# The half swap of a rotary embedding: one transfer set on ScalarE's queue in place of a product on TensorE

## The reference

```python
h = _layernorm(x) * (1.0 + scale) + shift            # scale, shift, gate = silu(c) @ w_ada + b_ada
p = h @ w_in[l]
u_f, z_f, cq, ckv, k_r, z_a = split(p)               # 1024, 1024, 512, 256, 64, 1024 columns
y_f = _fourier_mix(u_f, w_fmix[l]) * silu(z_f)
q = _rmsnorm(cq) @ w_q_b[l]                          # 8 heads of 128 + 64
kv = _rmsnorm(ckv) @ w_kv_b[l]                       # 8 heads of 128 + 128
q_rope = _apply_rope(q[..., 128:], cos, sin)         # 8 heads, 64 each
k_rope = _apply_rope(k_r, cos, sin)                  # one, shared by the heads
y_a = softmax((q_nope k_nope + q_rope k_rope) / sqrt(192)) v * silu(z_a)
x = _layernorm(ALPHA * x + gate * (concat(y_f, y_a) @ w_out[l]), g, b)

def _apply_rope(x, cos, sin):
    x1, x2 = split(x, 2, axis=-1)                    # halves of 32
    return concatenate([x1 * cos - x2 * sin, x2 * cos + x1 * sin])
```

## Time and profile before

| what | value |
|---|---|
| median of three runs | 1576.99 us (1576.58 to 1578.29) |
| span of the profiled execution | 1576.4 us |
| TensorE busy | 1505.3 us, 95% of the span |
| VectorE busy | 1064.3 us, 68% |
| ScalarE busy | 708.5 us, 45% |
| mean granted TensorE clock | 0.988 |
| moved by DMA | 345 MB, 219 GB/s over the span |
| the ten rotations' products on TensorE | 20 records (two each), 379 ns the median one |

### The profile page before, as it was taken

One profiled execution on the slowest core, in us unless ns is written; L12 is line 12 of the kernel. 1 busy time (PEld: TensorE's weight loads), 2 busy tenths in 40 slices (PEclk: granted clock), 3 DMA queues, 4 the chain that ended last, 5 costly groups with the idle time before them and its releaser, 6 DMA issues.

```text
span 1576.4 us, 25483 instructions
## 1 busy us (share of the span) xinstructions
PE 1505.3 (95%) x10143; PEld 1332.0 (84%) x10143; DVE 1064.3 (68%) x1729; ACT 708.5 (45%) x1216; POOL 40.7 (3%) x58
## 2 busy tenths in 40 slices
PE   5999999989979999999979999999998999999999
PEld 3678789987869788998859998889987998888987
DVE  3348588889987667577576683795655657766653
ACT  2334244334445445444435444454444546655442
POOL 3000000000000000000000000010000000000000
PEclk9999999999989999999999999999999999999999
DMA  9998888998837555776645554456664554434673
GB/s 356 406 407 305 277 292 316 358 351 331 332 100 263 188 192 180 253 251 205 199 151 183 171 166 144 146 181 196 188 197 148 162 160 122 123 118 134 188 219 102
DMA packets 101422, 345.04 MB, mean 219 GB/s; under 512 B 11216, under 2 KB 21684, under 8 KB 100536
## 3 DMA queue, kind: packets, MB, share of 16 engines
q1 hardware_dynamic: 96888, 327.42, 61.7%
q0 software_dynamic: 4416, 16.00, 3.0%
HBM read 341.17 MB, written 2.20 MB: 218 GB/s over the span
## 4 chain that ended last, share of the span: by engine, by line
PE 72%; DVE 12%; DMA 7%; ACT 5%; issue 4%; SPq 1%; DVEq 0%; ACTq 0%
PE PM L1478 60%; PE PB L1478 7%; DMA stg<-in_w_in 5%; DVE wlo L2181 2%; ACT whi L1862 2%; DVE AC L2094 2%; ACT AR L1862 2%; PE PB L1713 1%; DVE X L2094 1%; DMA stg<-in_w_ada 1%; DMA stg<-in_w_out 1%; SPq L1387 1%; PE PB L1685 1%; DVE SM L2444 1%; PE PB L1788 1%
## 5 line engine op out<-in xcount | busy, mean ns | idle before, releaser
L2181 DVE TENSOR_TENSOR wlo<-stg,whi 128x1024 fp32r<-128x1024 f32 (+2 forms) x417 | 498.0, 1204 | 346.4 <-ACT whi L1862 344.4
L1862 ACT ACTIVATE whi<-stg 128x1024 fp32r<-128x1024 f32 (+2 forms) x417 | 430.0, 1039 | 440.7 <-PE PM L1478 336.0
L1478 PE MATMUL PM<-Hh,whi 128*128 128x256 f32 x1824 | 527.9, 292 | 12.6 <-DVE wlo L2181 8.5
L1478 PE MATMUL PM<-Hh,wlo 128*128 128x256 f32 x1776 | 500.1, 284 | 0.0
L1478 PE MATMUL PM<-Hl,whi 128*128 128x256 f32 x1824 | 496.5, 284 | 0.0
L1478 PEld LDWEIGHTS PM<-Hh,whi 128*128 128x128 f32 x1824 | 351.8, 193 | 31.2 <-issue 16.3
L1478 PEld LDWEIGHTS PM<-Hh,wlo 128*128 128x128 f32 x1776 | 342.8, 193 | 0.0
L1478 PEld LDWEIGHTS PM<-Hl,whi 128*128 128x128 f32 x1824 | 341.4, 192 | 0.8 <-issue 0.2
L1478 PE MATMUL PM<-whi,Hh 128*128 128x512 f32 (+1 forms) x576 | 224.8, 391 | 0.9 <-DVE wlo L2181 0.5
L1478 PE MATMUL PM<-wlo,Hh 128*128 128x512 f32 (+1 forms) x576 | 221.4, 385 | 0.0
L1478 PE MATMUL PM<-whi,Hl 128*128 128x512 f32 (+1 forms) x576 | 218.9, 385 | 0.0
(11 more groups left out here) (279 smaller groups left out, 1420.1 us busy)
## 6 DMA issues: line engine op xcount, KB each, us to landing
stg<-in_w_ada SPq DMA_DIRECT2D x163, 512.0 KB, 6.2
stg<-in_w_in SPq DMA_DIRECT2D x105, 512.0 KB, 5.3
stg<-in_even_w_in SPq DMA_DIRECT2D x80, 512.0 KB, 3.6
stg<-in_odd_w_in SPq DMA_DIRECT2D x72, 512.0 KB, 3.5
stg<-in_w_out SPq DMA_DIRECT2D x64, 512.0 KB, 4.0
stg<-in_even_w_out SPq DMA_DIRECT2D x32, 512.0 KB, 3.6
stg<-in_odd_w_out SPq DMA_DIRECT2D x32, 512.0 KB, 3.6
AR<-in_w_ada SPq DMA_DIRECT2D x29, 512.0 KB, 15.1
```

The costliest lines, as they stand in the source:

```text
L1478: return e.matmul(out, l, r, start=start, stop=stop, skip_group_check=True)
L1862: return e.activation(out, x, f, **k)
L2181: e.tensor_tensor(wlo[s["slot"]][:, :, 0:n], stg[s["slot"]][:, :, 0:n], whi[s["hi"]][:, :, 0:n].bitcast(F32), ALU.subtract).then_inc(SEM[" ...
```

## The change

The product with `ROT` goes. In its place ScalarE issues four transfers from SBUF to SBUF, each of 32 partitions by 1 KB, which write the swapped block into `TMP`; the sign now lies in the sine table, since the constant for the angle is negative for the partitions whose half is the first. VectorE multiplies `TMP` by `SIN` in place. The PSUM bank isn't taken any more, `TMP` is taken before the transfers, and the step `rope` stands three yields behind them. Four transfers of one rotation count together on one semaphore (64), so the set before it must have landed in full before ScalarE issues the next.

```diff
         def rope(dst, x, name):
             yield
-            yield
-            b, fr = yield from self.take(self.banks)
-            mm = self.tick("rope_mm")
-            self.step("rope_mm", bank=b, free=fr, dst=dst, x=x)
-            yield
             i, ifree = yield from self.take(self.tmps)
+            before = ("rope_swap", self.count["rope_swap"]) if self.count["rope_swap"] else None
+            w = self.tick("rope_swap", 64)
+            self.step("rope_swap", dst=dst, x=x, tmp=i, tfree=ifree, before=before)
+            for _ in range(3):
+                yield
             a, c = self.tick("rope_sin"), self.tick("rope")
-            self.step("rope", bank=b, dst=dst, mm=mm, tmp=i, tfree=ifree, sin=a)
-            self.banks.put(b, a)
+            self.step("rope", dst=dst, swap=w, tmp=i, sin=a)
             self.tmps.put(i, c)
...
-        const, later = ("const_landed", 64), ("later_landed", 96)
+        const, later = ("const_landed", 64), ("later_landed", 80)
...
-                elif kind == "rope_mm":
-                    q.wait_ge(s["x"])
-                    q.wait_ge(later)
-                    q.wait_all(s["free"])
-                    e.matmul(B[:, 0:S], ROT[:, :], ar(s["dst"], S), start=True, stop=True).then_inc(SEM["rope_mm"], 1)
...
+                elif kind == "rope_swap":
+                    q.wait_ge(s["x"])
+                    q.wait_all(s["tfree"])
+                    q.wait_ge(s["before"])
+                    for r in range(0, 128, 32):
+                        o = r ^ 32
+                        e.dma_start(TMP[s["tmp"]][r:r + 32, 0:S], AR[o:o + 32, s["dst"]:s["dst"] + S]).then_inc(SEM["rope_swap"], 16)
...
                 elif kind == "rope":
                     T, dst = TMP[s["tmp"]], ar(s["dst"], S)
-                    q.wait_ge(s["mm"])
+                    q.wait_ge(s["swap"])
                     q.wait_ge(rope_tab)
-                    q.wait_all(s["tfree"])
-                    e.tensor_tensor(T[:, 0:S], B[:, 0:S], SIN[:, :], ALU.mult).then_inc(SEM["rope_sin"], 1)
+                    e.tensor_tensor(T[:, 0:S], T[:, 0:S], SIN[:, :], ALU.mult).then_inc(SEM["rope_sin"], 1)
...
-    c[:, 1664] = inv[p % 32]
+    c[:, 1664] = np.where(p % 64 < 32, -inv[p % 32], inv[p % 32])
```

More of the change, by code:

```diff
@@ L1272, in build @@
         ONE = sb("ONE", [128, 128])
-        ROT = sb("ROT", [128, 128])
         SWP = sb("SWP", [128, 128])
@@ L1419, in gpsimd @@
             for dst, src in (
-                    (ROT[:, :], cst[:, 128:256]), (CSS[:, :, :], cst[:, 384:896].rearrange("p (t n) -> p t n", t=2)),
+                    (CSS[:, :, :], cst[:, 384:896].rearrange("p (t n) -> p t n", t=2)),
                     (CF[:, :, :], cst[:, 1408:1664].rearrange("p (t n) -> p t n", t=2)),
@@ L2610, in constants @@
     c[:, 0:128] = np.eye(128)
-    for b in (0, 64):
-        for i in range(32):
-            c[b + 32 + i, 128 + b + i] = -1.0
-            c[b + i, 128 + b + 32 + i] = 1.0
     c[:, 256:384] = np.where(p[None, :] <= p[:, None], 0.0, NEG)
```

## The result

The changed kernel takes 1592.5 us (median of 4 runs, 1590.19 to 1595.09) against 1576.8 us: a ratio of 1.0094, with a 95% interval of 1.0082 to 1.0106. It is 15.7 us slower. I had forecast no measurable change.

A forecast was written before the change was run, and what follows sets the result against it. TensorE, busy 95% of the span, was taken to bound the kernel, with ScalarE met next. Layer 0 -0.3, layer 1's key -0.4 and its groups -0.2 gave -0.9 us: span 1575.5, with 0.6 added 1576.1 us; range 1573.0 to 1581.0.

The forecast's parts named there:

- What goes: TensorE loses ten products of 0.43 us and 1.8 us of waits for ScalarE: 6.1 us at most.
- rival A: All the time freed on TensorE is kept, ScalarE no longer stops it: up to 6.1 us, 1570.9; chance 0.12.
- Issuing: On ScalarE, 0.27 us an issue, 1.2 us a rotation with the wait for the copy; bounds 1.0 and 4.2.
- my own sum: Layer 1's keys' copy: VectorE's copy, transfers, split, copy: 592.42 + 1.2 + 1.06 + 0.66 = 595.34, 0.4 us later.
- that sum's first number: Layer 1: VectorE's copy of group 3 over at 592.42, as before; layer 1's groups taken at -0.2 us.
- Both engines are paced by TensorE before: Ahead of layer 1's scores: reason given that the gains of layer 0 (-0.3 us) and layer 1's key (-0.4) are kept.
- Landing: The swap's transfers, on ScalarE's queue beside the loads, land in 3.0 us; bounds 1.6 and 5.4.
- Rival B: ScalarE issues no set before the last landed; decides from 2.7 to 4 us of landing: +3.5, 1580.5; chance 0.24.
- The sign that I gave for B: VectorE or ScalarE waiting for `TMP`'s transfers by more than a microsecond in layer 1.
- Rival C: Slow issues on ScalarE, 1.06 us each, 4.2 a set: about +4, 1581; sign: over 0.6 us; chance 0.08.
- Layer 0: Fourier products 1.2 us earlier, keys 1.0 earlier; total between 1.0 earlier and 0.3 later, taken as -0.3.
- the "0.6 us": Amount by which the median of the runs lies above the profiled span of 1576.4, added to reach the forecast time.

The follow-up runs named there:

- GpSimd's copies: The change with four copies of 32 partitions on GpSimd in place of the four transfers issued by ScalarE: 1572.05 us, ratio 0.9969.
- The runs with the products kept: Kernel before, ScalarE also issuing four SBUF to SBUF transfers a rotation into a spare tile: 1593.3 us at the change's place, 1579.85 one to two rounds later.
- The exchanged copies: The change with two copies exchanged between engines: ScalarE makes `qr_out`, VectorE makes `q_out`: 1589.5 us, ratio 1.0083.
- Two semaphores: The change with one semaphore for each `TMP` buffer, so ScalarE doesn't wait for the set before to land: 1588.3 us, ratio 1.0065.
- the held copy: Kernel before; once, ahead of layer 1's first keys' copy, ScalarE issues a transfer and waits for it, three times: 1588.6 us, ratio 1.0075.
- two issues: Kernel before, products kept, ScalarE also issuing two transfers a rotation into a spare tile at the change's place: 1582.6 us, ratio 1.0032.
- later place with two semaphores: The change with the swap two rounds later, the rotation one, and one semaphore for each `TMP` buffer: 1578.6 us, ratio 1.0010.
- GpSimd's products: The change without transfers; GpSimd multiplies by the sine while swapping, VectorE only multiplies by the cosine and adds: 1574.7 us, ratio 0.9986.
- the later place: The change with the swap's step two rounds of the plan later and the rotation one round later: 1582.95 us, ratio 1.0036.

## Why the prediction was wrong, step by step

**What goes** was right. I had 0.43 us a product and the waits, 6.1 us at most, and rival A, all of it kept, at 1570.9. With nothing added on ScalarE (GpSimd's copies) the kernel takes 1572.05: 4.7 us. But that holds only while TensorE doesn't wait: where it waits for ScalarE anyway, the products stood inside the wait.

**Issuing: mis-sized.** I took 0.27 us an issue and 1.2 a set, from SyncE's row for a single partition. It is 0.612 and 2.45, inside my bounds of 1.0 and 4.2. Put into my own sum this gives layer 1's keys at 592.42 + 2.45 + 1.06 + 0.66 = 596.6, 1.6 us late. From VectorE's copy to the keys that is right: it took 1.8 us longer than before. But the keys came 9.8 us late, and the other 8.0 lie ahead of that sum: 4.8 from layer 0 and 3.2 from the turns.

**The step that failed** is that sum's first number. I wrote of VectorE's copy in layer 1 that one rotation fewer stands ahead of it "but the splits ahead of it come later, behind group 2's transfers", and let that be worth between 0.8 earlier and 0.4 later. I gave one set of transfers to the chain, the last. The traces show that the sets stand in a ring: each delays ScalarE's splits, these delay VectorE's low parts and its next copy, and that delays the next set. Group 0's was still covered (7.80 us to the next copy, 8.42 before); those of groups 1 and 2 were not (6.44 and 6.72 against 5.40 and 3.92). The copy that I took to end at 592.42 ended at 600.46. "Both engines are paced by TensorE before" was true of the kernel before and no reason for the one after. The runs with the products kept show that the place ahead of the splits is what counts, 16.4 against 3.0 us. The exchanged copies don't show that the ring over VectorE is worth only 3.0: with it cut, the wait for the landing held the sets.

**Landing: mis-sized.** 3.0 us against a median of 4.1, and 6.28 for the longest in layer 0's chain. Rival B said that ScalarE would be held by it, and from 2.7 to 4 us on. Two semaphores give 4.2 us where it had 4.4, but that agreement is luck: B put 3.9 of them into layer 1 and 0.5 into layer 0, and the traces show 2.26 us of waiting in layer 0 and 0.43 in layer 1, where the copies had come further apart, as its own "against" said. The sign that I gave for B, over a microsecond in layer 1, wasn't there.

**Rival C** said slow issues, 1.06 us each, and 1581. The issues were faster than that, though at 0.612 just above the 0.6 that I gave as its sign, and the time 11 us worse, by the same omission.

**Layer 0.** I expected a lead of 1.2 us at the Fourier products and 1.0 at the keys. The first became a lag of 0.56 us: the issues ran from 139.43 to 141.94, with the split and `u_out` behind them, and took more than the 2.1 us that TensorE had freed. At the scores the lag was 3.19. There I had 210.49 + 1.2 + 0.66 = 212.35; VectorE's copy ended at 211.07, group 3's set then waited 2.26 us for a landing of 6.28, went out in 2.55, and with the copy that gives 216.54. So the wait for the landing, which I put at nothing, and the size of the issues failed here, not the ring: the copies `qr_out` of layer 0 come 0.1 to 1.3 us late. Layer 0's 5.3 us were more than half of what the scores of layer 1 show. What I wrote of VectorE behind the scores had no test of its own; TensorE's wait at the gates is 4.46 us after 4.31.

**Left out entirely:** the granted clock. The two idle stretches cost 1.4 and 1.8 us beyond themselves, and the held copy showed the second by itself. Nor is the "0.6 us" what lies outside the span: in every later run of the kernel before the time is 2.1 to 2.3 us above the span, and in those of the change 1.8 to 1.9. By that the profiled execution before took about 1578.6 us (an estimate), above the median. The forecast itself isn't touched: -0.9 us from the median of 1576.99 is 1576.1 either way.

## What to carry to other kernels

When work moves to an engine that isn't the bottleneck, ask what stands behind it in that engine's order and what that feeds: here 24.5 us of issues cost 16.4 us ahead of the weight splits, and 3.0 one to two rounds later. Two waits that end together hide each other, so a run that removes one of them doesn't price it. Where your added work lies on a path that leads back to itself, don't take the next start from the old trace; go once around the ring for every repetition. A transfer isn't free to the engine that issues it, so issue it, or make the copy, where nothing waits.

## What the hardware showed that I had not expected

- Four issues of 32 partitions within SBUF take ScalarE 2.45 us (0.612 each in the middle); 32 partitions to HBM 0.442; a single one of 128 partitions within SBUF 0.472; and GpSimd issues the very same transfers in 0.496.
- Transfers of 32 KB beside loads of 512 KB land in 1.8 to 6.3 us, in the middle 4.1; in layer 1's stretch before, the loads took 4.3 and 5.4. In the run with the held copy the same transfer of 64 KB landed twice in 1.8 and once in 5.1 us.
- Whether the clock falls isn't told by the idle just ahead of the scores: 2.14 us came with scores of 4.65 us (two issues; 0.64 us of idle and one product stood ahead of it), 2.51 and 3.67 us (later place with two semaphores; exchanged copies, layer 0) with 3.06. What else decides wasn't settled.
- GpSimd's products and VectorE's sums at the same time took longer (828 against 425 ns in the middle for VectorE's; GpSimd's have no run alone to compare). With GpSimd's plain copies the sum stayed at 430.
- In the change and seven kernels made from it one of the ten sine products lasts 1.8 to 2.3 us in place of 0.42, with GpSimd's copies too, where there is no transfer. The traces show what stands beside it, in the change:

```profile
586.24 2.97 POOL L1441 TENSOR_TENSOR AC<-AC,stg 1x1024 f32<-1x1024 f32 x1 [127.21 <-DVE AC L2094]
...
587.21 2.29 DVE L2357 TENSOR_TENSOR TMP<-TMP,SIN 128x256 f32<-128x256 f32 x1
```

GpSimd adds a row of the bias to `AC`, and the product ends 0.29 us after it. In all eight kernels the long product is the one that starts while this addition runs, and it ends 0.27 to 0.29 us after it. With the later place no sine product meets it, and none is long. With the products kept none meets it either, and there the product reads `PB` in place of `TMP`. In the change VectorE's next low part follows at 591.32, and TensorE waits 0.32 us for it, so of the 1.9 us little reaches TensorE.
